# Second block's attentions with features on partitions, row blocks long and short in turn

## The reference

```python
h = rmsnorm(x, attn_norm_g)
fq, fk, fv, f_logit, sq, sk, sv = split(h @ w_in)         # 8 heads of 64 each, twice
# forgetting attention: q.k/8 + F[t] - F[s], F = cumsum(log_sigmoid(f)), s <= t, softmax, times v
# stick-breaking attention: z = q.k/8; A[t,s] = sigmoid(z[t,s]) * prod_{s<j<t} (1 - sigmoid(z[t,j])), s < t
o = concat([rmsnorm(o_fox, fox_out_g), rmsnorm(o_sb, sb_out_g)])   # each over 512 features
x = x + o @ w_out
h = rmsnorm(x, ffn_norm_g)
u = causal_dwconv(h @ w_up)                               # three taps
x = x + (silu(gate) * val) @ w_down
return rmsnorm(x, final_norm_g)
```

## Time and profile before

| | us |
|---|---|
| median of three runs | 1696.87 |
| profiled execution | 1700.36 |
| its span | 1698.5 |
| PE busy | 1633.2 |
| DVE busy | 883.5 |
| ACT busy | 645.4 |
| POOL busy | 366.1 |

### The profile page before, as it was taken

The page is one execution under the profiler, slowest core; times in us unless marked ns, Lnnn a source line. Parts: engine busy times, 40 slices in busy tenths (PEclk is TensorE's granted clock), DMA queues, the critical chain, the costliest instruction groups (busy, mean ns, idle before and its releaser), DMA issues.

```text
span 1698.5 us, 19241 instructions
## 1 busy us (share of the span) xinstructions
PE 1633.2 (96%) x7582; PEld 1292.9 (76%) x7582; DVE 883.5 (52%) x1401; ACT 645.4 (38%) x1106; POOL 366.1 (22%) x318
## 2 busy tenths in 40 slices
PE   5999998988999999999999999998999999999998
PEld 3566787766767788888888887775788888888886
DVE  5446555366357555444343324587564767777222
ACT  4332223355445433333322212466563444444222
POOL 3444214364012116111110205033202400000000
PEclk9999998999999999999999999999999999999999
DMA  6121112211221323233333322321102232332322
GB/s 231 51 74 37 50 55 75 87 57 56 75 63 50 112 88 98 92 95 99 99 100 94 94 98 70 112 63 38 44 7 76 86 98 90 97 99 87 124 88 73
DMA packets 39221, 139.51 MB, mean 82 GB/s; under 512 B 4331, under 2 KB 4971, under 8 KB 38940
## 3 DMA queue, kind: packets, MB, share of 16 engines
q1 hardware_dynamic: 39132, 138.29, 25.3%
HBM read 136.14 MB, written 2.10 MB: 81 GB/s over the span
## 4 chain that ended last, share of the span: by engine, by line
PE 83%; DVE 6%; POOL 5%; ACT 3%; issue 3%; DMA 1%; SPq 0%; POOLq 0%; DVEq 0%; ACTq 0%
PE ps L387 80%; PE ps L390 3%; POOL sqs L2105 2%; POOL sqt L2103 1%; DVE raw L1056 1%; ACT whi L1489 1%; DVE W L1307 0%; DVE wlo L863 0%; DVE T L1089 0%; DMA wraw<-in_ws 0%; DMA x<-in_x 0%; POOL Lb L2158 0%; DVE tp L1051 0%; DVE sd L962 0%; DVE raw L1043 0%
## 5 line engine op out<-in xcount | busy, mean ns | idle before, releaser
L863 DVE TENSOR_TENSOR wlo<-wraw,whi 128x1024 fp32r<-128x1024 f32 (+2 forms) x220 | 271.8, 1240 | 442.7 <-ACT whi L1489 442.0
L387 PE MATMUL ps<-hThi,whi 128*128 128x512 f32 x1128 | 455.0, 403 | 1.6 <-DVE skT L1394 0.9
L387 PE MATMUL ps<-hThi,wlo 128*128 128x512 f32 x1128 | 441.5, 391 | 0.0
L387 PE MATMUL ps<-hTlo,whi 128*128 128x512 f32 x1128 | 440.9, 391 | 0.0
L1489 ACT ACTIVATE whi<-wraw 128x1024 fp32r<-128x1024 f32 (+2 forms) x244 | 251.9, 1037 | 481.9 <-PE ps L387 467.9
L387 PEld LDWEIGHTS ps<-hThi,whi 128*128 128x128 f32 x1128 | 212.9, 189 | 57.5 <-issue 16.2
L387 PEld LDWEIGHTS ps<-hTlo,whi 128*128 128x128 f32 x1128 | 213.0, 189 | 45.5 <-issue 3.6
L387 PEld LDWEIGHTS ps<-hThi,wlo 128*128 128x128 f32 x1128 | 212.6, 188 | 45.3
L387 PE MATMUL ps<-whi,hThi 128*128 128x512 f32 (+1 forms) x224 | 90.1, 402 | 6.8 <-DVE wlo L863 6.8
L387 PE MATMUL ps<-whi,hTlo 128*128 128x512 f32 (+1 forms) x224 | 85.9, 383 | 0.0
L387 PE MATMUL ps<-wlo,hThi 128*128 128x512 f32 (+1 forms) x224 | 85.8, 383 | 0.0
(11 more groups left out here) (323 smaller groups left out, 2605.7 us busy)
## 6 DMA issues: line engine op xcount, KB each, us to landing
wraw<-in_ws SPq DMA_DIRECT2D x236, 512.0 KB, 3.5
x<-in_x SPq DMA_DIRECT2D x4, 512.0 KB, 7.5
x<-in_x SPq DMA_DIRECT2D x1, 2048.0 KB, 8.4
out<-ys SPq DMA_DIRECT2D x8, 256.0 KB, 2.2
dec<-in_dec SPq DMA_DIRECT2D x1, 1024.0 KB, 15.9
wraw<-in_ws SPq DMA_DIRECT2D x4, 256.0 KB, 2.6
vec<-in_vec SPq DMA_DIRECT2D x1, 788.0 KB, 4.7
w<-in_w SPq DMA_DIRECT2D x1, 512.0 KB, 14.3
```

Of the source, the lines that this page charges most:

```text
L387: return t.matmul(o, l, r, start=first, stop=last)
L863: v.tensor_tensor(wlo[h][:, 0:width(i)], wraw[h][:, 0:width(i)], whi[h][:, 0:width(i)].bitcast(F32), ALU.subtract).then_inc(lo_done[h], 1)
```

## The change

The unit order becomes block 3, 0, 2, 1 within each pair of heads, for both attentions. In stick-breaking GpSimd's addition moves to VectorE, behind the scan; the transposes take the sum, and ScalarE applies the exponential while it copies bank 6 to one of three `PT2`. The products with the values swap their operands: the values of a head are stationary, the weights moving, and the result has 64 features on partitions (0-63 for the even head, 64-127 for the odd one) and queries on columns; two heads are interleaved. In forgetting attention each row is divided by its sum ahead of the transpose (a reciprocal on VectorE in every step, the scaling on ScalarE for even units, on VectorE for odd ones), all transposes go to bank 6, all scores to banks 4 and 5.

Bank 7 then holds two heads for all 512 tokens, and is split into `ohi` and `olo` at once, not normalised. Squares are added over four pairs of heads (ScalarE, GpSimd), summed over partitions by TensorE, and the inverse root is spread as `Ro[0]` and `Ro[1]`. It is applied when `xs` and `xf` are evicted: each block is multiplied by `Ro` and then added to `xT`. So `xs` and `xf` no longer share banks; `xs` moves ahead of the drain with eight steps per slot, and `sv`, `fq`, `fk`, `fv` have rates 1, 3, 3, 3. `x_back` moves to the first slot and becomes transposes. Some semaphores are merged.

```diff
@@ build: buffers and unit order
 W5 = [sb(f"W5_{i}", AR + 112 + 2 * i, [128, 512]) for i in range(6)]
-PT2 = [sb(f"PT2_{i}", AR + 124 + 2 * i, [128, 512]) for i in range(2)]
+PT2 = [sb(f"PT2_{i}", AR + 120 + 2 * i, [128, 512]) for i in range(3)]
+osq = sb("osq", AR + 118, [128, 512])
+oss = [sb("oss0", AR + 126, [128, 512]), sb("oss1", AR + 114, [128, 512])]
+Ro = [sb("Ro0", AR + 112, [128, 512]), sb("Ro1", AR + 120, [128, 512])]
...
-s_units = [(n, h) for n in (3, 0, 2, 1) for h in range(8)]
...
+s_units = [(n, h) for j in range(4) for n in (3, 0, 2, 1) for h in (2 * j, 2 * j + 1)]
...
@@ tensor_program: group, norm and stick-breaking
+        if s == 0 and beside:
             beside(b, bank)
...
-def out_norm_turn(q, bank):
-    w.wait_ge(o_sc, 3 * q + 3)
+def head_squares(c, bank):
+    w.wait_ge(z_p, 5 * c + 3)
     take(bank)
-    for k in range(4):
-        op = across(bank, k, W5[5][:, k * 128:(k + 1) * 128])
-    op.then_inc(o_tr, 1)
-    free[bank] = [(o_lo, q + 1)]
+    for i in range(4):
+        op = mm(ps[bank][:, i:i + 1], oss[c][:, i * 128:(i + 1) * 128], ones[:, 0:1], True, True)
+    op.then_inc(z_mm, 1)
+    free[bank] = [(z_row, 2 * c + 1)]
...
+def head_roots(c, bank):
+    w.wait_ge(z_p, 5 * c + 5)
+    take(bank)
+    mm(ps[bank][:], ones[:], sqt[:], True, True).then_inc(z_mm, 1)
+    free[bank] = [(z_row, 2 * c + 2)]
...
-        w.wait_ge(s_w, u + 1)
+        w.wait_ge(s_sum, u + 1)
...
         n, h = s_units[u]
-        w.wait_ge(s_ev, u + 1)
+        w.wait_ge(s_ev, u + 2)
         w.wait_ge(sv_c, n + 1)
-        if h == 0:
+        if n == 3:
             take(7)
         for k in range(n + 1):
-            op = mm(ps[7][:, h * 64:(h + 1) * 64], PT2[u % 2][:, k * 128:(k + 1) * 128], sv[:, k, h * 64:(h + 1) * 64],
-                    k == 0, k == n)
-        op.then_inc(s_pv, 1)
-        if h == 7:
-            free[7] = [(o_c, u // 8 + 1)]
+            for i in range(2):
+                op = mm(ps[7][64 * i:64 * i + 64, n * 128:(n + 1) * 128], sv[:, k, (h + i) * 64:(h + i + 1) * 64],
+                        PT2[(u + i) % 3][:, k * 128:(k + 1) * 128], k == 0, k == n)
+                if k == n:
+                    op.then_inc(s_pv, 1)
+        if n == 1:
+            free[7] = [(o_lo, u // 8 + 1)]
...
@@ tensor_program: forgetting attention and order of the groups
-        wd, b = 128 * (pairs[u][0] + 1), 4 + u % 2
-        w.wait_ge(x_ex, u + 1)
-        take(b)
+        wd = 128 * (s_units[u][0] + 1)
+        w.wait_ge(x_sv if u % 2 else x_sa, u // 2 + 1)
+        take(6)
         for k in range(wd // 128):
-            op = across(b, k, Tf[u % 6][:, k * 128:(k + 1) * 128])
+            op = across(6, k, Tf[u % 6][:, k * 128:(k + 1) * 128])
         op.then_inc(x_tr, 1)
-        free[b] = [(x_ea if u % 2 else x_ev, u // 2 + 1)]
+        free[6] = [(x_ea if u % 2 else x_ev, u // 2 + 1)]
...
-        w.wait_ge(x_ea if u % 2 else x_ev, u // 2 + 1)
+        n, h = s_units[u]
+        w.wait_ge(x_ev, u // 2 + 1)
+        w.wait_ge(x_ea, u // 2 + 1)
         w.wait_ge(fv_c, 4)
-        if h == 0:
-            take(b)
+        if n == 3:
...
+            for i in range(2):
+                op = mm(ps[7][64 * i:64 * i + 64, n * 128:(n + 1) * 128], fv[:, k, (h + i) * 64:(h + i + 1) * 64],
+                        PTf[(u + i) % 4][:, k * 128:(k + 1) * 128], k == 0, k == n)
+                if k == n:
+                    op.then_inc(x_pv, 1)
+        if n == 1:
+            free[7] = [(o_lo, 4 + u // 8 + 1)]
...
+    for u in range(36):
+        while u == 5 and not fox_go:
             yield
+        if 3 <= u < 35:
+            turn(u - 3)
         if u < 32:
             scores(u)
-        if 3 <= u < 35:
-            turn(u - 3)
-        if u in (7, 22, 26):
-            out_norm_turn({7: 3, 22: 4, 26: 5}[u], 3)
-        if 5 <= u < 37:
+        if u == 5:
+            head_squares(0, 6)
+        if u == 9:
+            head_roots(0, 6)
+        if u >= 5 and u % 2:
...
+group("fq", hT, h_ready(2), lambda b: (h_v, 2 * (b // 2) + 2) if b % 2 else (h_a, 2 * (b // 2) + 2), 3)
+group("fk", hT, h_ready(2), lambda b: (h_v, 4 + 2 * (b // 2) + 2) if b % 2 else (h_a, 4 + 2 * (b // 2) + 2), 3)
...
+group("fv", hT, h_ready(2), lambda b: (fv_c, b + 1), 3)
 fox_go.append(True)
+for half in range(2):
+    group("xs%d" % half, lambda k: (ohi[:, k, :], olo[:, k, :]), lambda k, b: w.wait_ge(o_lo, k + 1),
+          lambda b: (e_s, 8 * half + 2 * b + 1), 8)
...
-for half in range(2):
-    group("xs%d" % half, lambda k: (ohi[:, k, :], olo[:, k, :]), lambda k, b: w.wait_ge(o_lo, 4), lambda b: None,
-          last=False)
-residual("xf%d", 3, lambda k: (ohi[:, 4 + k, :], olo[:, 4 + k, :]), lambda k, b: w.wait_ge(o_lo, 8), more=True)
+flow.beside.append(fox_norm())
+for half in range(2):
+    group("xf%d" % half, lambda k: (ohi[:, 4 + k, :], olo[:, 4 + k, :]), lambda k, b: w.wait_ge(o_lo, 4 + k + 1),
+          lambda b: (e_s, 16 + 4 * half + b + 1), 4)
...
-            mm(ps[bank][:, k * 128:(k + 1) * 128], xT[:, 4 * half + k, b * 128:(b + 1) * 128], ident, False, False)
+            t.matmul(ps[bank][:, k * 128:(k + 1) * 128], xT[:, 4 * half + k, b * 128:(b + 1) * 128], ident,
+                     start=k == 0, stop=False, is_transpose=True)
...
@@ vector_program
-            v.tensor_tensor(xT[:, f, :], p[:], xT[:, f, :], ALU.add).then_inc(e_x, 1)
+            if n == 3:
+                t = px[b % 2]
+                w.wait_ge(z_row, 4)
+                w.wait_ge(e_x, 16 + f - 1)
+                v.tensor_tensor(t[:], p[:], Ro[1][:], ALU.mult).then_inc(e_s, 1)
+                w.wait_ge(e_s, 16 + f + 1)
+                v.tensor_tensor(xT[:, f, :], t[:], xT[:, f, :], ALU.add).then_inc(e_x, 1)
...
+def head_low(q, gname):
     w.wait_ge(o_hi, q + 1)
-    for k in range(4):
-        op = v.scalar_tensor_tensor(olo[:, j0 + k, n * 128:(n + 1) * 128], ps[bank][:, k * 128:(k + 1) * 128], col(gname, k),
-                                    ohi[:, j0 + k, n * 128:(n + 1) * 128].bitcast(F32), ALU.mult, ALU.subtract)
-    op.then_inc(o_lo, 1)
+    w.wait_ge(o_sq, q + 1)
+    v.scalar_tensor_tensor(olo[:, q, :], ps[7][:], col(gname, q % 4), ohi[:, q, :].bitcast(F32), ALU.mult,
+                           ALU.subtract).then_inc(o_lo, 1)
...
+def head_roots(c, bank):
+    w.wait_ge(z_mm, 2 * c + 2)
+    v.tensor_copy(Ro[c][:], ps[bank][:]).then_inc(z_row, 1)
...
-    def evac(u):
-        wd = 128 * (s_units[u][0] + 1)
-        w.wait_ge(s_tr, u + 1)
-        if u >= 2:
-            w.wait_ge(s_pv, u - 1)
-        v.tensor_copy(PT2[u % 2][:, 0:wd], ps[6][:, 0:wd]).then_inc(s_ev, 1)
+        w.wait_ge(s_sc, u + 1)
+        v.tensor_tensor(L[:, 0:wd], zb[u % 3][:, 0:wd], nr[:, 0:wd], ALU.add).then_inc(s_sum, 1)
...
-        if 4 <= u < 36:
-            evac(u - 4)
...
+        if u >= 12 and u % 8 == 4:
+            head_low((u - 12) // 8, "gsb")
...
+    def shares(u):
+        wd, c, T = 128 * (s_units[u][0] + 1), u % 6, Tf[u % 6]
+        w.wait_ge(x_ex, u + 1)
+        v.reciprocal(st2[:, 16 + c:17 + c], st2[:, 8 + c:9 + c]).then_inc(x_rc, 1)
+        if u % 2:
+            w.wait_ge(x_rc, u + 1)
+            v.tensor_scalar(T[:, 0:wd], T[:, 0:wd], st2[:, 16 + c:17 + c], None, ALU.mult).then_inc(x_sv, 1)
...
-    def shares(q, n):
...
-        v.reciprocal(st2[:, 40:48], st2[:, c:c + 8]).then_inc(x_nv, 1)
...
-        v.tensor_tensor(heads(W5[3][:], 8), heads(ps[b][:], 8), st2[:, 40:48].unsqueeze(2).to_broadcast([128, 8, 64]),
-                        ALU.mult).then_inc(x_nv, 1)
...
+        if 3 <= u < 35 and (u - 3) % 2 == 0:
+            evac(u - 3)
         if u < 32:
             lowest(u)
-        if 3 <= u < 35 and (u - 3) % 2 == 0:
-            evac(u - 3)
...
+        if 1 <= u <= 32:
+            shares(u - 1)
+        if u == 5:
+            head_means(0, 6)
+        if u == 9:
+            head_roots(0, 6)
+        if u >= 11 and u % 8 == 3:
+            head_low(4 + (u - 11) // 8, "gfox")
...
+def projected(half):
+    def evac(b, p, done):
+        f, t = 4 * half + b, px[b % 2]
+        w.wait_ge(blocks, done)
+        w.wait_ge(z_row, 2)
+        if f >= 2:
+            w.wait_ge(e_s, 2 * f - 2)
+        v.tensor_tensor(t[:], p[:], Ro[0][:], ALU.mult).then_inc(e_s, 1)
+        w.wait_ge(e_s, 2 * f + 1)
+        v.tensor_tensor(xT[:, f, :], xT[:, f, :], t[:], ALU.add).then_inc(e_s, 1)
+    return evac
...
@@ scalar_program
+def head_high(q, gname):
+    w.wait_ge(s_pv if q < 4 else x_pv, 8 * (q % 4) + 8)
+    w.wait_ge(in_late, 32)
+    a.activation(ohi[:, q, :], ps[7][:], ACT.Copy, scale=col(gname, q % 4)).then_inc(o_hi, 1)
+    if q % 4 > 1:
+        w.wait_ge(z_p, 5 * (q // 4) + q % 4 - 1)
+    dst = osq if q % 4 else oss[q // 4]
+    a.activation(dst[:], ps[7][:], ACT.Square).then_inc(o_sq, 1)
...
-        L, wd = Lb[u % 5], 128 * (s_units[u][0] + 1)
-        w.wait_ge(s_sum, u + 1)
-        a.activation(L[:, 0:wd], L[:, 0:wd], ACT.Exp).then_inc(s_w, 1)
+        wd = 128 * (s_units[u][0] + 1)
```

(56 more changed lines are left out.)

243 lines of the change are left out of this document (96 added, 147 removed).

## The result

The changed kernel takes 1701.12 us (median of 20 runs, 1698.17 to 1704.56) against 1697.82 (1695.55 to 1700.42) of the kernel before on the same chips: ratio 1.0020, interval 1.0014 to 1.0026. It is slower by 3.3 us, where 1678 was forecast. Its profiled execution took 1699.2 us, with a span of 1697.0.

The account below looks back on a forecast made before the run. It took TensorE, busy 96% of the span, as what bounds the kernel; -14 - 10 + 6 + 0 + 2 - 3 = -19 from a median of 1696.87 gave 1677.9 us, range 1671 to 1684 (1662 to 1691 with the faster rivals).

Parts of the forecast that it names:

- Stick-breaking steps, -14: Stick-breaking stretch: of 18.5 us lost to TensorE's waits and slow clock, 4.5 remain, a gain of 14 us.
- Values, -10: Value products of both attentions: with operands swapped, two heads' column halves overlap on TensorE, saving 10 us.
- Columns don't overlap: Rival, chance 0.28: value products stay at 33.6 us, the total gain is 10 us, time 1687.
- Forgetting steps, +6: Forgetting attention beside w_out: VectorE at 90% or more adds 1.5 us to each slot, 6 us in all.
- its own signs of being wrong: TensorE waiting over 20 us beside the projection, or stick-breaking still idling for 10 us, would make the prediction wrong.
- Merging w_out with the drain, 0: w_out projection beside the forgetting steps: gives nothing itself, as the drain had no idle time to fill.
- Norm 0, end +2: Norm products replace transposes, net 0; waits behind the drain and at the squares cost 2 us together (0 to +4).
- Add-back, -3: Add-back as transposes: eight times from 0.81 to 0.44 us, a gain of 3.0 us.
- the forgetting steps run as one chain: Rival, chance 0.08 including milder forms: units don't overlap, steps cost their latency, +46 for +6, time 1718.

Follow-up runs that it names:

- the shorter chain alone: Kernel before with only stick-breaking's addition moved to VectorE and the exponential put behind the transposes, two PT2 buffers: 1688.51 us, ratio 0.9948 to the kernel before.
- the fastest kernel: Kernel before with the change's whole stick-breaking side and add-back, but old forgetting attention in the drain and w_out behind it: 1682.78 us, ratio 0.9908.
- the run with two banks: Changed kernel with w_out's first half behind the drain and odd units' transposes in bank 3: 1704.23 us, ratio 1.0043 to the kernel before.

## Why the prediction was wrong

By the steps of the sum, with the traces of before and after:

- **Stick-breaking steps, -14.** The mechanism was right and the size was off. TensorE's waits there fell from 12.8 to 8.1 us, the transposes from 11.7 to 9.2 us, the excess of projection products over 0.2265 us each by 0.2: 7.3 us in place of 14. The clock came back, from 0.96 to 0.99, but most of the waits stayed. The runs give 8.7 for the shorter chain alone. I had let the wait at bank 6 vanish with VectorE's copy; ScalarE's exponential took its place in the same order, behind its own queue.
- **Values, -10.** Right: 33.8 to 23.7 us. "Columns don't overlap" is refuted.
- **Forgetting steps, +6.** This is the step that failed. The stretch lost 14.3 us net; the values in it gained 3.8, and the norm products cost 0.5 more than the turns they replace, so the steps cost some 17.6. The forecast said: VectorE needs 14.7 us per eight steps against TensorE's 16.5, so each split or eviction in between is felt a little. The load itself had been put too high: 14.7 us for each of four slots are 58.8, and VectorE was busy for 47.5. Even so the steps took longer, because the comparison of the load of an engine with TensorE's time was the wrong one. The engines are in order, and a step passes through all three; the time is that of the lap, in which ScalarE's work and VectorE's work add up, with TensorE's score and transposes, instead of running beside each other. So both engines are idle for 43% and 49% of the stretch, and yet their added work costs most or all of its busy time. The normalisation costs 12.7 us for 14.4 of busy time on both, the second eviction operation 3.7 for 5.3, each taken away by itself and compared by the medians. In the traces of this stretch alone the two are worth 10.4 and 4.1 us of the 17.6. No run took both away, and no run isolates what is left.
- **Part of that is the clock.** Of the 17.6 us, 10.9 are waits of TensorE (0.8 to 11.7 us) and 6.7 are longer busy time. The granted clock in the stretch is 0.96, before it was 1.00; without the normalisation it was 1.00 again and 3.7 us of busy time went with it. The other 3.0 are not explained by any run. The forecast had no clock term in this stretch. That is also why its own signs of being wrong did not show: it named over 20 us of waiting beside the projection, or 10 us of idle time in stick-breaking, and these came to 11.7 and 8.1.
- **Merging w_out with the drain, 0.** Wrong: there was nothing to fill in the old drain, but the new steps left gaps. Beside them the projection is worth 7 us; without that the change would be at 1708. By the traces 1.4 us of this are waits that it filled, and the rest goes with a clock that stayed higher.
- **Norm 0, end +2.** Norm about right: in the two stretches the turns are 2.9 us less and the new products 2.0 more. The mask products behind the scores take 1.0 us more, which I had not counted. The end is +3.1 up to the token sums, mostly the wait of 2.87 for GpSimd's chain, plus some 1.7 for the slow products behind it: over the bound of +4. In the fastest kernel, whose second half of w_out has one eviction operation and no head norm, that wait is 0.6 again.
- **Add-back, -3.** Right: 2.9 alone.

As measured the terms add up to -7.3 - 10.1 + 17.6 - 0.9 + 1.0 + 4.8 - 2.9 = +2.2, against +3.3 by the medians. All but the last are read from one execution of each kernel, and one kernel's stick-breaking stretch differed by 1.6 us between two executions.

The rival that came nearest was "the forgetting steps run as one chain", which had a chance of 0.08. It was right in kind and too strong in degree: it put a whole unit's latency into a step, and 1718. I set it aside because of six T buffers, four PTf buffers and scores issued ahead. Buffers let work start early; they do not let an operation overtake the one ahead of it in its queue. The fastest kernel shows it from the other side, with the forgetting half undone. The kernel before took 1698.4 us on its chip; less 7.3 for the stalls, 6.3 for the values of that half and 2.9 for the add-back, plus 1.0 for the mask products, that is 1682.9, and it took 1682.8. So close an agreement is luck, since its four executions lie between 1680.0 and 1683.2, but no large term is missing.

Not settled: why the shorter chain still leaves 6.2 us of waits at bank 6; and how much of its gain is the shorter chain, and how much that GpSimd's additions no longer slow VectorE, since the run changed both at once. Two of the six (2.4 us) lie by GpSimd's scaling of Qf and ScalarE's copies of it, but no run took these away. Moving the low part so that VectorE needn't wait for ScalarE's square was not tried.

## What to carry to other kernels

Between engines with queues in order, don't compare an engine's load with the bound engine's time. Follow one lap, from an instruction of the bound engine through every queue back to its next dependent instruction, and count everything that stands ahead on each queue. Here work added there cost most or all of its busy time although both engines were half idle, half of it as waits and half as a lower clock, and the same work placed one step later cost 48 us more. When a change has two halves, look at each half's stretch by itself: the one that had 12.8 us of waits to lose gained, the one with 0.8 could only get new ones, and the first half alone is 16 us faster where both together are 3 slower. And read busy time and granted clock beside the waits: an order of work that looks as if it filled gaps may be worth more by the clock that it keeps up.

## What the runs showed of the hardware

Two 64-column halves of TensorE overlap for float32 products where their products alternate. 16 passes of 128 moving columns take 1.03 us when two heads take turns, 1.51 when they come one after the other, and 1.72 as products with 128 stationary and 64 moving columns. The change of shape has a small price: the two mask products between scores and values rose from 0.28 to 0.37 us, where the values behind them are in halves, and stayed at 0.28 where other products follow. The Trainium skill ("TensorEngine Tiling (Array Packing)", "Key Properties") says that a change of mode drains the array; 0.09 us more ahead of the first value product fits with that, though no trace shows the drain itself.

In three places the granted clock was 1.00 in the stretch that held TensorE's stall and fell in the next, with TensorE busy again. In the run with two banks the 18 us from 1218 on have a granted clock near half (1.2 of 2.4 GHz), with TensorE busy throughout, after six microseconds in which it was busy for 4.07:

```profile
1206.00:1212.00 6.00, 6.00 (x33) 4.60 (x32) 2.10 (x2) 3.66 (x6) 1.29 (x1) 1.00 0.10 38
1212.00:1218.00 6.00, 4.07 (x16) 2.54 (x14) 2.29 (x10) 3.56 (x9) 0.00 (x0) 1.00 0.27 87
```
```profile
1218.00:1236.00 18.00, 17.90 (x64) 10.81 (x66) 7.20 (x30) 7.76 (x24) 2.06 (x2) 0.53 0.00 0
```

At a clock of 0.53 those 18 us do what 9.5 us do at full clock, so by this estimate a stall of 2 us cost over 8 more. In the changed kernel it is milder: 3.94 us of work from 1217 to 1223, then a clock of 0.72 for six. The third place is the wait of 2.87 us for GpSimd's squares, with 0.52 for the 3.5 us behind it.
